# A hybrid decoder trunk on one core: the state-space layer's lead-in in another order, and first scores from a gained but unnormalised X

## The reference, cut to what matters

```python
def s5_mixer(h, ...):
    step = exp(log_step); mag = exp(lam_re * step)
    lb = mag * (cos(lam_im * step), sin(lam_im * step))          # complex
    coef = (lb - 1) / lam
    bu = u @ (coef * b)                                          # by group of 16 channels
    s = associative_scan(s[t] = lb * s[t-1] + bu[t])
    y = gelu(re(s @ c) + d_skip * h)
    val, gate = split(y @ w_glu)
    return val * sigmoid(gate)

def peer_ffn(h, w_q, sub_keys, u_tab, v_tab):                    # 8 heads
    q = h @ w_q
    s = q @ sub_keys                                             # 2 x 128 scores a head
    best, idx = top 16 of the sums of the top 16 of each half
    gate = softmax(best)
    act = h . u_tab[idx]
    return sum(gate * gelu(act) * v_tab[idx])                    # 128 experts a position

for layer in (0, 1):
    x = x + (s5_mixer, attention)[layer](rms_norm(x, norm_mix[layer]))
    x = x + peer_ffn(rms_norm(x, norm_ffn[layer]))
```

## Time and profile before

| what | value |
|---|---|
| median of 3 runs | 1725.62 us (1724.81 to 1733.73) |
| the profiled execution's own time | 1723.77 us |
| its span in the trace | 1721.7 us |
| busy: PE, DVE, ACT, POOL | 1293.6, 1096.1, 599.1, 608.9 us |
| moved by DMA | 682.78 MB, mean 397 GB/s |
| mean granted TensorE clock | 0.865 of full |

### The profile page before, as it was taken

One profiled execution on the slowest core, in us unless ns is written; L12 is line 12 of the kernel. 1 busy time (PEld: TensorE's weight loads), 2 busy tenths in 40 slices (PEclk: granted clock), 3 DMA queues, 4 the chain that ended last, 5 costly groups with the idle time before them and its releaser, 6 DMA issues.

```text
span 1721.7 us, 19404 instructions
## 1 busy us (share of the span) xinstructions
PE 1293.6 (75%) x6612; PEld 552.4 (32%) x6612; DVE 1096.1 (64%) x2608; ACT 599.1 (35%) x2024; POOL 608.9 (35%) x549
## 2 busy tenths in 40 slices
PE   4986766577969868997878796799788677645554
PEld 4573211122713323333345231443253233200000
DVE  9767888744568666435447976653474848676544
ACT  5143432323243245114333332531362523234222
POOL 6014544443242234223333322322343234444441
PEclk9989878688979988997899898999898778868777
DMA  9079999999999999999999999999999999999996
GB/s 375 20 297 402 360 415 408 417 423 422 422 423 416 423 420 421 424 425 416 415 422 417 408 422 423 411 396 426 421 391 424 400 382 411 423 405 410 419 421 286
DMA packets 85923, 682.78 MB, mean 397 GB/s; under 512 B 9792, under 2 KB 10176, under 8 KB 11584
## 3 DMA queue, kind: packets, MB, share of 16 engines
q0 software_dynamic: 73728, 536.90, 75.9%
q1 hardware_dynamic: 12096, 144.64, 20.1%
HBM read 680.46 MB, written 1.05 MB: 396 GB/s over the span
## 4 chain that ended last, share of the span: by engine, by line
PE 37%; DMA 33%; DVE 17%; ACT 7%; issue 4%; POOL 2%; ACTq 0%; POOLq 0%; DVEq 0%
DMA ringmem<-experts,lay 23%; PE ps L495 13%; PE ps L556 12%; DMA wt<-w_qkv 9%; DVE ringmem L1461 6%; PE ps L571 5%; POOL ringmem L1432 2%; ACT lay L1112 2%; ACT S L1009 2%; PE ps L729 1%; PE ps L901 1%; PE ps L508 1%; PE ps L855 1%; PE ps L887 1%; DMA wt<-w_glu 1%
## 5 line engine op out<-in xcount | busy, mean ns | idle before, releaser
L1432 POOL DMA_INDIRECT ringmem<-experts,lay x512 | 580.3, 1133 | 1043.6 <-PE ps L495 899.3
L495 PE MATMUL ps<-ringmem,S 128*32 128x512 f32 x2048 | 620.5, 752 | 359.3 <-ACT S L1009 356.4
L1461 DVE CUSTOM_DVE_ANT_0 ringmem<-ringmem,Hrep 128x1024 f32<-128x1024 f32 x384 | 461.8, 1224 | 257.5 <-DMA ringmem<-experts,lay 255.4
L495 PEld LDWEIGHTS ps<-ringmem,S 128*32 128x32 f32 x2048 | 111.9, 125 | 755.0 <-ACT S L1009 505.0
L556 PE MATMUL ps<-wt,hT 128*128 128x512 f32 x576 | 258.2, 601 | 19.0 <-DMA wt<-w_qkv 18.9
L1004 ACT ACTIVATE gelus<-dots 128x2 f32<-128x2 f32 x224 | 45.1, 201 | 559.3 <-DVE dots L1461 553.0
L1461 DVE CUSTOM_DVE_ANT_0 ringmem<-ringmem,area 128x1024 f32<-128x1024 f32 x128 | 155.3, 1225 | 97.8 <-DMA ringmem<-experts,lay 95.5
L556 PEld LDWEIGHTS ps<-wt,hT 128*128 128x128 f32 x576 | 107.3, 191 | 171.4 <-issue 165.4
L991 ACT ACTIVATE S<-con,lay 128x32 f32<-128x32 f32 x512 | 134.6, 311 | 44.9 <-PE ps L495 44.1
L1009 ACT ACTIVATE S<-S,gelus 128x32 f32<-128x32 f32 x512 | 136.6, 314 | 24.5 <-ACT gelus L1004 1.1
L571 PEld LDWEIGHTS ps<-hT,wt 128*128 128x128 f32 x896 | 107.5, 201 | 16.1 <-issue 15.9
(11 more groups left out here) (270 smaller groups left out, 1183.6 us busy)
## 6 DMA issues: line engine op xcount, KB each, us to landing
wt<-w_qkv SPq DMA_DIRECT2D x36, 2048.0 KB, 11.6
wt<-w_q SPq DMA_DIRECT2D x14, 2048.0 KB, 11.6
wt<-w_glu SPq DMA_DIRECT2D x5, 2048.0 KB, 11.7
ringmem<-experts,lay POOLq DMA_INDIRECT x512, 12.5
wt<-w_o SPq DMA_DIRECT2D x4, 2048.0 KB, 11.8
...
```

What stands on the lines that cost most here:

```text
L495: last = pe.matmul(ps[TG * t:TG * (t + 1), half, :], S[:, u % 2, i, :], ring[:, (2 * u + i) % RING, D + half * 512:D + (half + 1) * 512], ...
L1432: pool.indirect_dma_start(ring[:, s % RING, :], None, experts[phase // NC], bass.IndirectOffsetOnAxis(ap=rows[:, phase % NC, j, n:n + 1], ...
L1461: last = v.tensor_tensor_reduce(ring[:, i, 0:D], ring[:, i, 0:D], hrep(phase, j), 1.0, 0.0, ALU.mult, ALU.add, dots[:, b, second:second + 1])
```

## The change

It touches the lead-in alone, on all five engines. What it does:

- Turns of tiles 1 to 3: ACT makes the products (`turns`, eight small operations a tile) and rounds up by adding a large constant (`round_up`), DVE subtracts in one operation (`part_of_turn`). POOL has no part in it any more. The clearing of `CL` goes from POOL to the head of DVE's queue.
- Planes of C by tile: POOL makes them for one tile at a time (`c_planes`), tile 0 before the scans and tile m + 1 after `last_state(m)`. ACT places and PE convolves one tile at a time (`place_c`, `conv_blocks(m)`, `take_conv`), in a part of PSUM bank 2 that ACT clears (`open_conv`).
- DVE: `s5_norms` goes between the sum of squares and the root; `s5_lb(0)` goes ahead of `s5_coef`, which has fewer, wider operations; `s5_lb(1)` goes behind the first scan. The spread numbers of tiles 2 and 3 are copied by ACT into the rows of X of chunk 1 (`LAMS`), which are loaded later in turn, as is the first item of query weights (it waits for the last tile's convolution).
- ACT: `root(0)` goes ahead of the copy of `lamT`; `gelu_y` of blocks 0 and 1 stands between the tables of tiles 1 and 2.
- The last tile is rotated and scanned in two halves, and y of block 6 waits for the first alone. PE's order of `glu_first`, `s5_bu` and `s5_y` is new.
- H for the first scores is X times the norm weights, written half by half as X is added up; `turn_halves` takes it. The first row root is applied to H later (`root0`), and in the exponential of the gates of phase 0.
- `first_scores`: the ring's block 2 is projected between the two halves of `spread_first`, block 3 behind `g.at(0, 1)`, and quarter 1 behind `g.at(0, 3)`. `norm_scale` of chunk 1 and `g.at(0, 2)` stand ahead of DVE's `top_k(FIRST[1])`, and ACT's `gate_quarter(FIRST[1])` behind its copy of the queries of quarter 3.

```diff
+        def produced(c, k):
+
+            return (ST + 1) * c + k // 2 + 1 + (c == 0 and k == KT - 1)
...
                     if n == 0:
-                        sp.wait_ge(conv_done, 1)
+                        sp.wait_ge(conv_done, ST)
...
+            sp.wait_ge(lb_ready, ST)
             sp.dma_start(X[:, 1, :], x[P:2 * P, :]).then_inc(x_in[1], 16)
...
-            def s5_bu(c, m):
+            def s5_bu(c, m, parts=(1, 0)):
...
+            def conv_blocks(m):
+
+                if m == 0:
+                    pe.wait_ge(bs_in, 16)
+                pe.wait_ge(conv_open, m + 1)
+                pe.wait_ge(cw_ready, 4 * m + 2)
+                for i in range(2):
...
-                pe.wait_ge(prod_ready, ST * c + m + 1)
-                if k == 0 and c == 0:
-                    pe.wait_ge(cw_ready, 8)
-                    pe.wait_ge(conv_ready, 1)
+                pe.wait_ge(prod_ready, produced(c, k))
+                if i == 0 and c == 0:
+                    pe.wait_ge(cw_ready, 4 * (m + 1))
+                    pe.wait_ge(conv_ready, m + 1)
...
-            def glu_first(k, based):
+            def glu_first(k):
 
                 pe.wait_ge(y_gelu, k + 1)
                 for i in (2, 0, 3, 1):
                     if k == 0:
                         pe.wait_ge(glu_in[i], 16)
-                        pe.wait_ge(lb_ready, ST)
+                        pe.wait_ge(lam_copied, ST - 2)
+                        pe.wait_ge(lb_ready, 2)
                     if i == 1:
-                        if based <= KT:
-                            pe.wait_ge(y_base, based)
+                        if k < KT - 2:
+                            pe.wait_ge(conv_open, k // 2 + 2)
+                        elif k == KT - 2:
+                            pe.wait_ge(y_base, KT)
...
-                spread_first()
+                spread_first(range(QUAD))
+
+                def ring_block(i):
+                    pe.wait_ge(wq_in[i - 2], 16)
+                    project_turned(None, BANKS0[i], done=wq_used, w=wq_ring[i - 2])
+
+                ring_block(2)
+                spread_first(range(QUAD, 2 * QUAD))
                 project_turned(item(0, 0, WQ0), BANKS0[0], parts=(2, 3))
                 score(2, BANKS0[0], 0, (2, 3))
+                g.at(0, 1)
                 pe.wait_ge(best_ready, 1)
-                for i in (2, 3):
-                    pe.wait_ge(wq_in[i - 2], 16)
-                    project_turned(None, BANKS0[i], done=wq_used, w=wq_ring[i - 2])
-                g.at(0, 1)
+                ring_block(3)
+                g.at(0, 2)
                 score(3, BANKS0[2], 2)
                 score(4, BANKS0[3], 3)
-                g.at(0, 2)
+                g.at(0, 3)
                 project_turned(item(0, 0, WQ0 + 1), BANKS0[1])
-                g.at(0, 3)
                 score(5, BANKS0[1], 1)
...
-                pe.wait_ge(lb_ready, 2)
                 lam_to_channels(2)
+                s5_bu(0, 1, (1,))
+                pe.wait_ge(hT_ready, norm_event(0, 0, 0) + 1)
+                conv_blocks(0)
+                pe.wait_ge(lam_copied, 1)
                 lam_to_channels(3)
-                s5_bu(0, 1)
-                pe.wait_ge(hT_ready, norm_event(0, 0, 0) + 1)
-                conv_blocks()
                 s5_y(0, 0)
+                s5_bu(0, 1, (0,))
                 s5_y(0, 1)
-                s5_bu(0, 2)
-                glu_first(0, 3)
-                s5_y(0, 2)
-                glu_first(1, 4)
-                s5_y(0, 3)
-                s5_bu(0, 3)
-                for k in range(4, KT):
-                    glu_first(k - 2, k + 1)
-                    s5_y(0, k)
-                    if k == KT - 2:
-                        pe.wait_ge(bu_used, ST)
-                        for n in range(k - 1):
-                            glu_rest(n)
-                glu_first(KT - 2, KT + 1)
-                for n in range(KT - 3, KT - 1):
+                for m in range(1, ST):
+                    glu_first(2 * m - 2)
+                    glu_first(2 * m - 1)
+                    conv_blocks(m)
+                    if m + 1 < ST:
+                        s5_bu(0, m + 1)
+                    s5_y(0, 2 * m)
+                    if m + 1 < ST:
+                        s5_y(0, 2 * m + 1)
+                glu_first(KT - 2)
+                pe.wait_ge(bu_used, ST)
+                for n in range(KT - 1):
                     glu_rest(n)
-                glu_first(KT - 1, KT + 1)
+                s5_y(0, KT - 1)
+                glu_first(KT - 1)
                 first_scores()
 
             def layer0(gphase, c):
+                pe.wait_ge(hrep_ready, 2 * QUAD)
...
+                act.activation(gex[:, heads[0]:heads[1]], gex[:, heads[0]:heads[1]], ACT.Exp,
+                               scale=root0 if ph == 0 else 1.0).then_inc(gate_exp, 1)
...
+            def turns(m):
+
+                if m == 1:
+                    act.wait_ge(lam_dve, 2)
+                for q in range(PPT):
+                    for i in range(2):
+                        n = PPD * m + 2 * q + i
+                        last = act.activation(sinT[:, PPT * m + q, HALF * i:HALF * (i + 1)], ramp[:, 0:HALF],
+                                              ACT.Copy, scale=frac[:, n:n + 1])
+                link(last)
+                q = slice(PPT * m, PPT * (m + 1))
+                act.activation(cosT[:, q, :], sinT[:, q, :], ACT.Identity,
+                               bias=round_up[:, 0:1]).then_inc(whole_ready, 1)
+
...
+                if between is not None:
+                    between()
+                act.activation(sinT[:, q, :], sinT[:, q, :], ACT.Sin,
+                               scale=-TWO_PI if m else TWO_PI).then_inc(tab_act, 1)
+
+            def copy_lam(m):
+
+                act.wait_ge(lam_spread, m + 1)
+                act.copy(LAMS[m - 2], ps[:, 0, :]).then_inc(lam_copied, 1)
...
+            def place_c(m):
+
+                act.wait_ge(c_ready, 2 * (m + 1))
...
+            def take_conv(m):
+
+                act.wait_ge(conv_done, m + 1)
+                act.copy(conv[:, 2 * m:2 * m + 2, :].rearrange("p k c -> p (k c)"),
+                         ps[:, 2, 0:HALF]).then_inc(conv_ready, 1)
+                act.wait_ge(conv_ready, m + 1)
+                base_y(0, 2 * m)
...
+                    if c == 0 and k % 2:
+                        open_conv(k // 2 + 1)
+                    else:
+                        base_y(c, k + 1)
...
-                table(0)
-                copy_half(0, 0, 0)
+                table(0, lambda: copy_half(0, 0, 0))
                 copy_half(1, 0, 0)
+                turns(1)
                 spread_mag(0)
+                act.wait_ge(y_open, 1)
+                open_conv(0)
+                copy_lam(2)
+                turns(2)
+                act.wait_ge(zeroed, 7)
+                act.wait_ge(cl_zeroed, 1)
+                place_c(0)
+                act.wait_ge(skip_in, 16)
+                take_conv(0)
                 table(1)
+                copy_lam(3)
+                spread_mag(1)
+                turns(3)
+                gelu_y(0, 0)
+                gelu_y(0, 1)
                 table(2)
-                act.wait_ge(zeroed, 7)
-                place_c(0)
-                place_c(1)
-                act.wait_ge(skip_in, 16)
-                act.wait_ge(y_open, 1)
-                base_y(0, 0)
-                spread_mag(1)
                 table(3)
-                act.wait_ge(conv_done, 1)
-                act.copy(conv[:, :, :].rearrange("p k c -> p (k c)"), ps[:, 3, 0:32 * KT]).then_inc(conv_ready, 1)
-                place_c(2)
-                place_c(3)
-                for k in range(KT):
-                    gelu_y(0, k)
-                    if k in (1, 3):
-                        spread_mag(2 + k // 2)
+                for m in range(1, ST):
+                    place_c(m)
+                    take_conv(m)
+                    if m + 1 < ST:
+                        spread_mag(m + 1)
+                    gelu_y(0, 2 * m)
+                    gelu_y(0, 2 * m + 1)
...
-                spread_h()
+                spread_h(range(QUAD))
                 gate_quarter(*FIRST[0])
+                spread_h(range(QUAD, 2 * QUAD))
                 act.wait_ge(w_used, item(0, 0, WQ0) + 1)
                 copy_q(0, BANKS0[0], slice(2, 4))
-                gate_quarter(*FIRST[1])
-                act.wait_ge(wq_used, 1)
+                g.at(0, 1)
                 act.wait_ge(score_done, 2)
                 copy_q(2, BANKS0[2])
-                g.at(0, 1)
+                g.at(0, 2)
                 act.wait_ge(wq_used, 2)
                 copy_q(3, BANKS0[3])
+                gate_quarter(*FIRST[1])
...
+            root(0)
             act.wait_ge(lam_turned, 1)
             act.copy(lamT.rearrange("p r n -> p (r n)"), ps[0:PAIRS, 0, 0:2 * P]).then_inc(lamT_ready, 1)
-            root(0)
...
+            def c_planes(m):
+
+                pairs = slice(PPD * m, PPD * (m + 1))
```

(74 more changed lines are left out.)

226 lines of the change are left out of this document (120 added, 106 removed).

## The result

The changed kernel takes 1740.51 us (median of 10 runs, 1728.80 to 1744.87) against 1728.28 for the kernel before on the same chip (1723.03 to 1733.73): a ratio of 1.0060, 95% interval 1.0042 to 1.0078, so by the ratio some 10 us slower. The prediction had 1726.5, 0.9 above no change, and a range of 1718 to 1732. The profiled execution has a span of 1739.0 us.

The account below looks back on a forecast made before the run. It took DMA as full nearly all the time, with DVE at quarter 1 setting the gathers' position. Lead-in -5.3, order +4.9, slow projection start +1.4 gave +0.9 us: 1726.5 on the scale of the runs' median, range 1718 to 1732.

Parts of the forecast that it names:

- what decides: At quarter 1's first part, DVE sets the gathers' position, not the first gather's start; forecast 147.7 against 146.8 us.
- F: Start of the first gather, end of the lead-in; forecast at 105.0 us, against 110.37 before.
- the head start of gathers 4 and 5: Ring block 2, projected 15 us earlier, frees these gathers; a pause of some 4 us before 150 spends the gain.
- its own sign: Stated test at quarter 1: the prediction is wrong if it opens before 143 or after 152 us.
- -5.3 at the first gather: Lead-in term: the projection starts at 87.2 instead of 92.52, and the first gather moves with it, 5.3 us earlier.
- PE sets its end: Lead-in's end: PE's `glu_first` blocks decide, with the last `glu_rest` over at 81.9 against 86.42 us, gain 4.5.
- gather 3 landed: F + 12.7; its dot product 1.2: F + 13.9: First step from F to quarter 1: 1.9 us to first bytes, four gathers of 2.5, 0.8 tail, then DVE's dot product.
- the chain as I wrote it: First gather to quarter 1: landing, top-k, gates, step pair, products, projection, scores; F + 41.3, 4.9 us more than before.
- a slow start: Projection of quarter 1 behind PE's new 6 us pause: 1.4 us added to 7.41, giving quarter 1 at F + 42.7.
- The bound for the projection: Projection of quarter 1: between 7.4 us and 5 us more at the slow pace throughout, written as 11.7.
- the two rows: Trace rows for PE's projections: 32 instructions took 5.83 us after a pause, 64 took 7.41 in the middle of work.
- a cost between 0 and 9 us: Bounds given for the later part, from the first gather to quarter 1.
- PE never speeds up: Rival in the lead-in: waits keep PE slow, four `glu_first` cost 13.2 us, +14 in all, 1740 us; chance 0.06.

Follow-up runs that it names:

- e6: e1, but ring block 2 projected between the halves of the spread of H, so gathers 4 and 5 start early; 1721.70 us, ratio 0.9989.
- e1: Changed kernel with the old order of the first scores put back on PE, ACT and DVE, new lead-in kept; 1721.94 us, ratio 0.9966.
- e4: Kernel before, with its old lead-in, given only the changed kernel's order of the first scores; 1742.79 us, ratio 1.0094.
- e8: e1 with the last tile rotated and scanned whole instead of in two halves; 1719.34 us, ratio 0.9976.
- e3: Changed kernel with SP's GLU weights of chunk 1 held back until the dot products of slots 2 and 3; 1730.92 us, ratio 1.0008.
- e5: e1 with ACT's two copies of H's halves put ahead of the root; 1715.30 us, ratio 0.9951.
- e2: Changed kernel with the projection of quarter 1 moved ahead of `g.at(0, 3)` on PE; 1727.84 us, ratio 1.0006.
- e10: Changed kernel with the edits of e2 and e3 together; 1726.03 us, ratio 0.9991.
- e9: e1 with H again made behind the root and the gate's exponential without its scale; 1717.40 us, ratio 0.9971.
- e11: e5 with GLU weights of chunk 1 held back until the dot products of slots 2 and 3; 1720.13 us, ratio 0.9956.

## Why the prediction was wrong

**Right: what decides.** That the first part of quarter 1, and not the first gather, sets the position of the stream, is borne out by all eleven kernels: gather 64 follows quarter 1 within 3.4 us, over a range from -10.0 to +14.7, while F alone misleads by 17.5 (4.2 earlier in the changed kernel, whose gather 64 starts 13.3 later). That the head start of gathers 4 and 5 is spent again agrees with e6, which is no faster than e1. By its own sign, quarter 1 after 152, the prediction was wrong: 157.1.

**Right: the lead-in.** Forecast -5.3 at the first gather, measured -4.2 in the changed kernel, and 5.9 us on the whole time (e1 against before, e4 against changed). Forecast and shown too: PE sets its end, not the last scan (e8). That the last `glu_rest` ended at 82.9, with 81.9 forecast, is in part luck. Scan 2 was over 2.9 us earlier than forecast, so that DVE had a lead of 4.7 us there over the kernel before and still 1.6 at the last scan's end, where I had 1.8 and none. But blocks 4 and 5, which follow it on PE, ended at 70.4, with 70.2 forecast: PE ran at its slower pace over most of block 4 (last section), which I had not counted. The two errors cancel.

**Wrong: "gather 3 landed: F + 12.7; its dot product 1.2: F + 13.9".** The dot product of slot 3 started at F + 21.2 and ended at F + 22.4, 8.5 us later. The term counted four gathers of 2.5 us as if they had the DMA engines alone. SP's 2.62 MB were issued 4.4 us behind F, gathers 4 and 5 at 5.5 and 6.8. e3 takes the 2.62 MB out and has slot 3's dot product start at F + 14.2, 7.0 us earlier and 1.5 behind the F + 12.7 forecast. An estimate of the size agrees: four gathers and the 2.62 MB are 6.8 MB, at the 389 GB/s of 108.00 to 127.40 us 17.5 us, with 1.9 and 0.8 at the ends F + 20.2. Gathers 4 and 5 can have little part in it: in e5 gather 4 starts only at F + 11.4, SP's transfer runs as in the kernel before, and slot 3 is taken at F + 20.8.

I had named neither SP's issue nor what it is released by, although it was there before (at 111.69, F + 1.3) and the trace of the kernel before shows what it does to the landing. Its dot product of slot 3 waits for the gather too, until F + 21.0:

```profile
131.35 1.22 DVE L1461 CUSTOM_DVE_ANT_0 ringmem<-ringmem,Hrep 128x1024 f32<-128x1024 f32 x1 [1.09 <-DMA ringmem<-experts,lay]
```

There nothing on the path to quarter 1 waited for it, since head 2's top-k had gone ahead. The change put that top-k, and with it the gates, the products and the projection, behind this landing. With F + 21.0 read from this row in place of F + 12.7, the chain as I wrote it would have come to 8.3 us more.

**The rest of that chain** was close: top-k 9.5 (9.3), gate 3.5 (3.5), step pair 2.7 (2.6). PE's products behind the 10.46 us pause took 3.5 instead of 1.9, the projection and its scores together 9.3 instead of 10.1 plus the 1.4 for a slow start. Sum of these: 8.5 + 0.2 + 0.1 + 1.6 - 0.8 - 1.4 = 8.2, against 8.3 between F + 51.0 and F + 42.7. That the slow pace cost about what I had put down for it is luck in part: it fell on other instructions. (The bound for the projection is 11.7 us, which is 4.3 more than 7.4 and not 5.)

**The clock.** TensorE does run at the slower pace behind the pause of 10.46 us, as the two rows had it: the granted clock is 0.51 from 144.30 to 147.84, its lower level of 1.2 GHz, and 1.00 from 147.84 to 155.00. The Trainium skill, "TensorE: Matmul & The Clock Gate", Part 1, has the throttled state as the default and activity releasing it; the trace agrees. But here the eight product instructions ahead of the projection took the slow stretch, and the projection had its full pace (7.41). In e4 a part of the projection was slow as well (8.53).

**The chances.** I gave the order a cost between 0 and 9 us, where it costs 14.6 from F to quarter 1, and had no case in which the transfers land late. A landing later by the 8.5 us measured, in the chain as it was written, gives 0.9 + 8.5 = 9.4, near the measured 10. The rival "PE never speeds up" named 1740, almost the time measured, but for another reason: its 13.2 us were to be lost in the lead-in, which gained 4.2.

**What the order would have needed.** A repair on PE (e2) or at SP (e3) makes the changed kernel neutral, both together too (e10, its interval spans 1); but no kernel with it was faster than e1, and the early gathers that it buys brought no gain by themselves either (e6). The lowest ratio has the changed lead-in with the old order and the root behind the copies (e5), 8.5 us faster than before; the intervals of e1, e8, e9 and e11 overlap with its own.
